# The inner rows of three feed-forward nets turned by VectorE and DRAM instead of TensorE, with three changes at the kernel's start

## The reference, cut to what matters

```python
def swiglu(x, w_gu, w_down):          # x: 256 x 1024, w_gu: 1024 x 5632, w_down: 2816 x 1024
    g, u = jnp.split(x @ w_gu, 2, axis=-1)
    return (jax.nn.silu(g) * u) @ w_down
```

## Time and profile before

| | us |
|---|---|
| median of three runs | 905.39 |
| the profiled execution | 905.16 |
| its span, first instruction to last | 903.4 |
| TensorE busy | 893.8 |
| VectorE busy | 614.2 |
| ScalarE busy | 460.2 |
| DMA, GB/s over the span | 219 |

### The profile page before, as it was taken

How to read it: one execution, slowest core, us unless ns; L and a number is a source line. 1 busy time by engine, 2 the same in 40 slices (tenths; PEclk the granted TensorE clock), 3 DMA queues, 4 the chain that set the end, 5 groups by cost and what they waited for, 6 DMA issues and landing times.

```text
span 903.4 us, 11262 instructions
## 1 busy us (share of the span) xinstructions
PE 893.8 (99%) x4208; PEld 746.9 (83%) x4208; DVE 614.2 (68%) x862; ACT 460.2 (51%) x695; POOL 42.2 (5%) x66
## 2 busy tenths in 40 slices
PE   9999999999999999999999999999999999999996
PEld 7888888888998888888888888888888888888885
DVE  6778977647558877587677777765768755555643
ACT  6675543626588466447544444454445344444530
POOL 0010000022103000000000000001000100000000
PEclk9999999999999999999999999999999999999999
DMA  9897778774554444444687777765755565555531
GB/s 360 327 347 279 275 268 295 265 226 150 187 176 173 172 179 163 163 164 154 229 292 279 280 264 279 282 246 172 248 187 166 198 219 187 186 187 186 184 120 47
DMA packets 56575, 197.83 MB, mean 219 GB/s; under 512 B 6936, under 2 KB 7880, under 8 KB 56392
## 3 DMA queue, kind: packets, MB, share of 16 engines
q1 hardware_dynamic: 55944, 196.19, 62.5%
q10 hardware_dynamic: 576, 0.92, 0.3%
HBM read 196.01 MB, written 1.07 MB: 218 GB/s over the span
## 4 chain that ended last, share of the span: by engine, by line
PE 96%; DVE 2%; issue 1%; ACT 0%; DMA 0%; POOL 0%; POOLq 0%; ACTq 0%
PE ps L708 29%; PE ps L710 29%; PE ps L709 29%; PE ps L735 2%; PE ps L646 1%; PE ps L623 1%; PE ps L834 1%; PE ps L850 1%; PE ps L616 1%; DVE t_wl L1183 0%; PE ps L792 0%; PE ps L826 0%; PE ps L774 0%; DMA t_acc<-in_xT 0%; PE ps L841 0%
## 5 line engine op out<-in xcount | busy, mean ns | idle before, releaser
L1183 DVE TENSOR_TENSOR t_wl<-t_raw,t_wh 128x1024 fp32r<-128x1024 f32 (+3 forms) x308 | 361.2, 1204 | 106.5 <-ACT t_wh L892 104.5
L892 ACT ACTIVATE t_wh<-t_raw 128x1024 fp32r<-128x1024 f32 (+3 forms) x308 | 307.4, 1040 | 87.4 <-DMA t_raw<-in_f_up 39.2
L708 PE MATMUL ps<-t_wh,t_XH 128*128 128x512 f32 (+2 forms) x640 | 250.7, 392 | 0.0
L710 PE MATMUL ps<-t_wh,t_XL 128*128 128x512 f32 (+2 forms) x640 | 247.1, 386 | 0.0
L709 PE MATMUL ps<-t_wl,t_XH 128*128 128x512 f32 (+2 forms) x640 | 246.7, 386 | 0.0
L710 PEld LDWEIGHTS ps<-t_wh,t_XL 128*128 128x128 f32 x640 | 120.1, 188 | 24.3
L709 PEld LDWEIGHTS ps<-t_wl,t_XH 128*128 128x128 f32 x640 | 120.3, 188 | 22.5
L708 PEld LDWEIGHTS ps<-t_wh,t_XH 128*128 128x128 f32 x640 | 120.2, 188 | 22.4
L708 PE MATMUL ps<-t_wh,t_YH 128*128 128x512 f32 x288 | 113.5, 394 | 0.2 <-DVE t_YL L1603 0.2
L710 PE MATMUL ps<-t_wh,t_YL 128*128 128x512 f32 x288 | 112.2, 390 | 0.0
L709 PE MATMUL ps<-t_wl,t_YH 128*128 128x512 f32 x288 | 112.1, 389 | 0.0
(11 more groups left out here) (227 smaller groups left out, 629.2 us busy)
## 6 DMA issues: line engine op xcount, KB each, us to landing
t_raw<-in_f_up SPq DMA_DIRECT2D x131, 512.0 KB, 4.0
t_raw<-in_f_dn SPq DMA_DIRECT2D x66, 512.0 KB, 3.6
t_raw<-in_ada SPq DMA_DIRECT2D x48, 512.0 KB, 3.6
t_raw<-in_mkv SPq DMA_DIRECT2D x8, 512.0 KB, 3.5
t_raw<-in_ga SPq DMA_DIRECT2D x8, 512.0 KB, 3.2
t_raw<-in_gc SPq DMA_DIRECT2D x8, 512.0 KB, 3.2
t_raw<-in_gb SPq DMA_DIRECT2D x8, 512.0 KB, 3.7
t_raw<-in_wo SPq DMA_DIRECT2D x8, 512.0 KB, 3.2
```

Source lines behind the costliest of these rows:

```text
L708: pe.matmul(o, xh, h, start=k == 0, stop=False)
L710: x = pe.matmul(o, xl, h, start=False, stop=k == n - 1)
L892: act.activation(wh[:, m % SPL, lo:w], raw[:, n % RAW, lo:w], ACT.Copy).then_inc(hi_made, 1)
L1183: dve.tensor_tensor(wl[:, n % RAW, lo:w], raw[:, n % RAW, lo:w], wh[:, m % SPL, lo:w].bitcast(F32), ALU.subtract).then_inc(drained, 1)
```

## The change

The step `hid_turn` is gone. In its place stand four steps per four groups (q = 0 to 5, the last with two half-size groups that are left):

- `blocks` on DVE: one `transpose` instruction turns `hp` (now 128 x 1024 for two groups and both row blocks) into `tp`, within blocks of 32x32 only.
- `spill` on SP: four DMAs, one for each band of 32 partitions, write `tp` to a buffer in DRAM (512 KB).
- `reload` on SP: one DMA reads it back with the bands spread so that 128 inner rows stand on partitions, into `tp`. It waits for `spilled`.
- `inner` on ACT and DVE: two copies for `HH` and two subtractions for `HL`, now read from `tp` in SBUF.

For q = 0 to 4 `spill` stands at unit 8q+8, `reload` at 8q+9, `inner` at 8q+12 (43 for q = 4); for q = 5 at 44, 45 and 48. A DMA's run is 128 values, 512 bytes (256 bytes for q = 5). The rows of the downward weights are put in a matching order on the host. At the start, ACT's queue now fetches unit 1 too, the unused transposes are 15 instead of 12, ACT's first instruction is a SiLU, and the row statistics, the first group's SiLU and the conditioning row come one step earlier.

```diff
+    def inner(f, u):
+        return [(step, f, q) for q in range(6) for step, late in (("spill", 0), ("reload", 1), ("inner", 3 if q == 4 else 4))
+                if u == (8 * q + 8 if q < 5 else 44) + late]
...
-                own = [("hid_turn", f, g - 2), ("hid_turn", f, g - 1)] if g and g % 2 == 0 and i == 2 else []
-                unit(f"{f}_up{g}", i, *own, *extra.get(4 * g + i, ()))
+                unit(f"{f}_up{g}", i, *inner(f, 4 * g + i), *extra.get(4 * g + i, ()))
             if (f, g) != ("f1", 0):
                 S.append(("hid", f, g))
+            if g % 2 or g == 10:
+                S.append(("blocks", f, g // 2))
...
-                for _ in range(12):
+                for _ in range(15):
                     pe.transpose(ps[:, 3, 0:P], ident[:, :], ident[:, :])
...
-            def hid_turn(f, g):
-                s = g % 2
-                b = bank(("hid", f, g), *hid_lo.at(f, g))
-                for t in (0, 1):
-                    pe.wait_ge(*hid_made.at(f, g, t))
-                    for c in (0, 1):
-                        m = pe.transpose(ps[:, b, c * 256 + t * P:c * 256 + t * P + P], hp[:, s, t, c * P:c * P + P], ident[:, :])
-                m.then_inc(turned, 1)
...
+                name, i = STREAM[1]
+                act.dma_start(raw[:, 1, :], A[name][i]).then_inc(landed[1], 16)
...
-                act.activation(col("first"), mhalf[:, 0:1], ACT.Copy)
+                act.activation(col("first"), mhalf[:, 0:1], ACT.Silu)
...
+            def inner(f, q):
+                act.wait_ge(reloaded, 16 * (inner_no(f, q) + 1))
+                for t in (0, 1):
+                    act.activation(parts_of(HH, q, t), placed(q, t), ACT.Copy).then_inc(*hid_hi.by(f, q, t))
...
+            def blocks(f, q):
+                n = inner_width(q) // 2
+                dve.wait_ge(*hid_made.at(f, 2 * q + (q < 5), 1))
+                dve.transpose(tp[:, 0:2 * n].rearrange("p (t n) -> p t n", t=2), hp[:, :, 0:n]).then_inc(*blocked.by(f, q))
+            def inner(f, q):
+                for t in (0, 1):
+                    dve.wait_ge(*hid_hi.at(f, q, t))
+                    dve.tensor_tensor(parts_of(HL, q, t), placed(q, t), parts_of(HH, q, t).bitcast(F32),
+                                      ALU.subtract).then_inc(*hid_lo.by(f, q, t))
...
+            def spill(f, q):
+                n = inner_width(q)
+                sp.wait_ge(*blocked.at(f, q))
+                for i in range(4):
+                    rows = inner_rows[i, :, :, 0:n // 8].rearrange("b f e -> f b e")
+                    sp.dma_start(rows, tp[32 * i:32 * i + 32, 0:n].rearrange("f (b e) -> f b e", b=8)).then_inc(spilled, 16)
+            def reload(f, q):
+                n = inner_width(q)
+                sp.wait_ge(spilled, 64 * (inner_no(f, q) + 1))
+                rows = inner_rows[:, :, :, 0:n // 8].rearrange("i (t j) f e -> (j f) (i t) e", t=2)
+                sp.dma_start(tp[:, 0:n].rearrange("p (b e) -> p b e", b=8), rows).then_inc(reloaded, 16)
```

More of the change, by code:

```diff
@@ L180, in ups @@
                     continue
[L181 to L182 removed]
+                unit(f"{f}_up{g}", i, *inner(f, 4 * g + i), *extra.get(4 * g + i, ()))
             if (f, g) != ("f1", 0):
                 S.append(("hid", f, g))
+            if g % 2 or g == 10:
+                S.append(("blocks", f, g // 2))
     def downs(f, extra, tail):
         for i in range(11):
[L188 removed]
+            unit(f"{f}_dn0", i, *inner(f, 44 + i), *extra.get(44 + i, ()))
         S.extend(rows(f, 0, 0) + rows(f, 0, 1))
@@ L502, in build @@
         silu_made, hid_made = Signal(sem("silu"), both(hid_keys)), Signal(sem("hid"), both(hid_keys))
-        hid_hi, hid_lo = Signal(sem("hid_hi"), hid_keys), Signal(sem("hid_lo"), hid_keys)
+        inner_keys = [(f, q) for f in FFNS for q in range(6)]
+        blocked = Signal(sem("blocked"), inner_keys)
+        hid_hi, hid_lo = Signal(sem("hid_hi"), both(inner_keys)), Signal(sem("hid_lo"), both(inner_keys))
+        spilled, reloaded = sem("spilled"), sem("reloaded")
         halves = steps("half")
@@ L573, in out_of, with inner_no, inner_width, placed @@
                             "ukv0": "kv0", "ukv1": "kv1"}.get(name, name), t)
+        def inner_no(f, q):
+            return 6 * FFNS.index(f) + q
+        def inner_width(q):
+            return 1024 if q < 5 else 512
+        def placed(q, t):
+            n = inner_width(q)
+            return tp[:, 0:n].rearrange("p (i t c n) -> p t c i n", i=4, t=2, n=32)[:, t]
+        def parts_of(a, q, t):
+            return a[:, 4 * q:4 * q + inner_width(q) // 256, t * P:t * P + P].rearrange("p c (i n) -> p c i n", i=4)
         def psum_2(bank):
@@ L967, in hid @@
                                    scale=r).then_inc(*silu_made.by(f, g, t))
-            def hid_turn(f, g):
-                b, full = place["hid", f, g]
-                act.wait_ge(turned, full)
-                act.activation(HH[:, 2 * g:2 * g + 2, :], psum_2(b), ACT.Copy).then_inc(*hid_hi.by(f, g))
+            def inner(f, q):
+                act.wait_ge(reloaded, 16 * (inner_no(f, q) + 1))
+                for t in (0, 1):
+                    act.activation(parts_of(HH, q, t), placed(q, t), ACT.Copy).then_inc(*hid_hi.by(f, q, t))
             def squares(p, j, t):
@@ L1298, in hid @@
                     if g >= 2 and t == 0:
-                        dve.wait_ge(turned, place["hid", f, g - 2][1])
+                        dve.wait_ge(*blocked.at(f, g // 2 - 1))
                     if f == "f3":
@@ L1619, in _ @@
             part = {"split": split, "ada": ada, "xpart": xpart, "front": front, "mem_part": mem_part, "rope1": rope1, "rope2": rope2, "rope3": rope3, "rope5": rope5, "ada_sum": ada_sum, "ada_rows": ada_rows,
-                    "hid": hid, "hid_turn": hid_turn, "half": half, "rms": rms, "gain": gain, "scaled": scaled_, "nturn": nturn, "nsplit": nsplit,
+                    "hid": hid, "blocks": blocks, "inner": inner, "half": half, "rms": rms, "gain": gain, "scaled": scaled_, "nturn": nturn, "nsplit": nsplit,
                     "xturn2": xturn2, "mk_stat": mk_stat, "lat_stat": lat_stat, "lat_row": lat_row, "lat_turn": lat_turn,
@@ L1747, in consts_ @@
                 fetch_x(1, 1)
-                for n in range(1, RAW):
+                fetch_x(2, 2)
+                for n in range(2, RAW):
                     if n < 4:
@@ L1825, in _ @@
                     "load_cond": load_cond, "ada_rows": ada_rows, "load_mod": load_mod,
-                    "load_mid": load_mid, "gate": gate, "load_final": load_final, "final": final}
+                    "load_mid": load_mid, "gate": gate, "load_final": load_final, "final": final, "spill": spill, "reload": reload}
             for name, *args in SCHEDULE:
@@ L1863, in ffn @@
             add(f"{tag}_up{j}", np.concatenate([g[:, j], u[:, j]], 1))
-        halves(f"{tag}_dn", down)
+        down, n = f(down), 5 * 512
+        quads = down[:n].reshape(5, 4, 4, 32, D).transpose(0, 2, 1, 3, 4).reshape(n, D)
+        last = down[n:].reshape(4, 2, 32, D).transpose(1, 0, 2, 3).reshape(256, D)
+        halves(f"{tag}_dn", np.concatenate([quads, last], 0))
     a["x"] = f(i["x"])[0].reshape(2, P, D)
```

22 lines of the change are left out of this document (9 added, 13 removed).

## The result

The changed kernel takes 895.01 us (median of 4 runs, 894.64 to 895.74), the kernel before 905.28 us beside it (4 runs, 904.44 to 905.69). The ratio is 0.9889 with a 95% interval of 0.9872 to 0.9906: 10.3 us faster, and 5.2 us slower than the forecast of 889.8. That is outside the forecast's own 888.0 to 892.0, and 0.5 us inside the upper end of the wide range. The profiled execution has a span of 892.9 us against 903.4.

What follows compares the result with a forecast made beforehand. TensorE, busy 893.8 of 903.4 us, was taken as the bound. 905.16 - 14.5 + 0.5 - 1.6 = 889.6, and 0.23 us to the median: 889.8 us, own range 888.0 to 892.0, wide range (8 in 10) 887.0 to 895.5.

Steps and rivals of the forecast that it cites:

- step A: On TensorE in all three nets: removing the transposes of the inner rows saves 14.5 us.
- VectorE's transpose at 1.2 us and its cover: On VectorE: the 128x1024 transpose takes 1.2 us (bounds 0.9 and 2.4), hidden behind the matmuls, cost 0.
- the middle of the nets: Away from the start of f1: ScalarE's wait for the reload and SP's blocked fetches cost 0.
- 12 us of slots: With `ada`, a refetch 18 us ahead, less landing and both splits, leaves 12 us as cushion.
- Rival 1: In f1 and f2: transfers become the bound at 341 GB/s, some 6 us lost, 896 us; chance 0.13.
- the empty stretch of 2.4 us: In each cycle: at most 2.4 us in which the DMA queue may stand empty while SP waits for written rows.
- step B: Beginning of f1, unit 17: 5.2 us of delay against 4.3 in hand, 0.5 us lost (bounds 0 and 5).
- 4.3 us in hand: At unit 17 of f1: VectorE had it at 50.5 us, TensorE takes it at 54.8, before the change.
- step C: At the start: TensorE's clock rises earlier for three more transposes, 1.6 us less (bounds 0 and 2.4).

Runs made afterwards that it cites:

- the doubled spill: The changed kernel with each spill of f2 and f3 written twice, the second copy to DRAM rows nobody reads: 897.91 us, ratio 0.9919.

## Why the prediction was right or wrong

**Right: step A, 14.5 us from TensorE.** The leads show it, fifteen steps of 0.87 to 0.89 us and three of 0.45, and eight units take 21.8 us in all three nets. That TensorE's busy time fell by 14.5 us too is partly chance: the earlier clock at the start took some 1.3 us off it and the half clock at unit 17 put 1.7 on. With the stand out of the way the whole of it arrives: the kernel with nothing of `q` = 0 of f1 on the queue is 904.79 - 889.00 = 15.8 us faster, which is A and some 1.3 us from the start and small parts. The Trainium skill's rule in "VectorE: DVE Perf Modes", section "Rules for kernel authors", to use TensorE for a 128x128 transpose if a PSUM destination will do, would have kept these 14.5 us in the time; the measurement decides against it where TensorE is the bound.

**Right: VectorE's transpose at 1.2 us and its cover.** Rows by form of the changed kernel:

```profile
L1332 DVE STREAM_TRANSPOSE t_tp<-t_hp 128x1024 f32<-128x1024 f32 x15 | 18.7, 1245 | 0.5
...
L1332 DVE STREAM_TRANSPOSE t_tp<-t_hp 128x512 f32<-128x512 f32 x3 | 2.1, 711 | 0.1
```

1.245 us. The forecast put f1's fullest stretch at 21.7 of 21.8 us; it has 21.45, and TensorE waits for nothing in it.

**Right: the middle of the nets, though with less to spare than forecast.** The spill's parts land after 3.4 us and the reload after 5.2 (forecast: 2.4 to 4, and 4, and under 5 as a sign). ScalarE waited 34.2 us for the reload in 14 times, 2.4 us in the mean and 9.3 at the longest, more than the 0 to 2 us of the forecast; no unit of TensorE behind unit 18 came late for it. The forecast compared this with 4.11 us as the longest wait for TensorE's turn; that is the longest in the rows shown, and over the whole kernel before it was 5.4 us, in 18 waits of 67.9 us. The small packets were priced about right: the queue's busy time rose from 0.625 x 903.4 to 0.697 x 892.9 us of 16 engines, 924 us x engine, for 38,160 packets more: 24 ns each, where 30 had been taken. The cycle was forecast at 341 GB/s and the rows say 346 and 349 in f1, 334 in f2. What was too high is the cushion in f2: the forecast counted 12 us of slots, the trace shows 5.3 us in the middle of the net and 3.2 at the tightest unit, and the doubled spill used it up. Rival 1 (transfers the bound) did not come true, but it was closer than its 0.13 with "12 us less 12" made it look.

By the limit of some 358 GB/s for one core in the Trainium skill ("DMA: Bandwidth & Descriptors", section "Bandwidth") and the empty stretch of 2.4 us each cycle would have been 1.4 us too long. The cycles had no wait. At 334 to 349 GB/s they lie under that figure and do not test it by themselves, but the changed kernel moved 417 GB/s in the row from 56.6 to 60 us above. The same section of the Trainium skill gives some 358 GB/s as the share when both cores of a domain stream, and 425 for one alone; the rows agree with the latter.

**Wrong: step B, the supply of f1, taken as 0.5 us and measured at 6.0.** The place, the unit and the mechanism were named; the size was not. The prediction compared 4.3 us in hand with 5.2 us of new delay, the bytes and TensorE's earlier arrival, and booked 0.5. What it had wrong:

- SP's own wait at the spill was not in the sum at all, only in its upper bound, and there by half. SP stood 4.8 us, since the product it waits for stood behind the conditioning row. Alone it makes unit 17's low part 3.1 us later. This is the step that failed.
- The bytes were taken as 2.7 us and are worth 2.7 us alone: right. But both together make it 6.7 us later, 0.9 more than their sum.
- The stand brought the clock down: 3.4 us at 1.2 GHz, 1.7 us more. The prediction priced a wait as its length.

With SP's 3.1 us in it the sum would have been 8.3 us against 4.3, 4.0 late, near the upper bound of 5 that was given. The mistake was to go near the lower end of 0 to 5, although the sign of SP's wait is known: the code makes SP wait for a product, and the trace of before has that product late. SP issued the memory rows, which the spill now precedes, from 32.45 on, and VectorE made the product only at 34.36:

```profile
34.36 0.87 DVE L1304 SCALAR_TENSOR_TENSOR t_hp<-ps,t_sc,t_sg 128x256 f32<-128x256 f32 x2
```

**Half right: step C, 1.6 us at the start.** The mechanism holds: in the changed kernel the first unit's matmuls were 0.23 us apart from 6 us on, and unit 4 started at 16.83 instead of 18.29, 1.46 us earlier, against 1.6 forecast. But alone it measured 0.7 us in the time. In one profiled execution the clock rose only at 11.1 us with the same fifteen transposes, when the first unit's high part came late and TensorE stood 0.61 us before it. And in the changed kernel it was worth nothing, since what TensorE gained it stood longer at unit 17. The forecast added C to B as if they were independent; the prediction had itself counted C against the 4.3 us in hand, and then booked it as a gain all the same.

**The sum.** By the table of leads: the start 1.46, fifteen pairs and three single groups 14.6, small parts 0.5, less 4.79 and 1.33 at units 17 and 18, is 10.4 of the 10.5 us by which the span fell. The forecast had 1.6, 14.5, nothing, and 0.5 us. That 895.01 us still lies inside 887.0 to 895.5 owes something to luck: the range reached that high for rival 1, transfers as the bound in f1 and f2, and what took the time was one stand of TensorE.

**A version that beats both.** The first inner group two units later: 889.86 us, 5.1 us under the changed kernel, with everything computed; with the conditioning row early as well 889.77, which can't be told from it. 0.8 to 0.9 us over the kernel without that group is all that is left there. The small loads stay where they are in it. Moving them only moved the stand; what stays open is how such a load would have to be written to cost less, which no run tried.

## What to carry to other kernels

When work is moved from the bound engine to queues, the steady state is the easy part; look for the one fetch that has the least time in hand, and add up every delay that the change puts ahead of it, the new waits of the issuing engine among them, before deciding that it "about fits". Delays that cost under 1 us alone cost 6 us together once the cushion is gone, and a gain upstream of such a place is worth nothing until it is mended. To measure such delays, compare when the fetched data is ready, not how long the bound engine waits. An issuing queue that is made to wait for a product should do so where that product is long made: two units later was nearly the whole repair.

## What the runs showed of the hardware that was not expected

- The norm rows, the positions and the rotation's row are 48 KB and less each, and yet while they land the 16 DMA engines stand nearly idle: 0.04 of the time and 5 GB/s from 42.5 to 44.5 us in the kernel before, 0.03 and 3 GB/s from 48.3 to 49.5 in the changed one, against 421 and 424 GB/s once the fetches behind them run. The packets in these stretches are the 64-byte ones of the two loads that copy one row of 16 values to 128 partitions. Moved away from it, the five loads gave unit 17's fetch 3.2 us back.
- The issue of the DMA that followed a spill, the memory rows and a reload on SyncE's queue took 2.76 to 4.25 us in seven kernels, whether it was a small load or, in the kernel with the norm rows late, a fetch of weights (2.96 us). In the kernels that leave the spill and the reload out, the same small load took 0.45 us. SP can fetch nothing meanwhile.
- A matmul stream that stood 4.3 us came back at 1.2 GHz and ran so for 3.4 us, 1.7 us more. After stands of 2.7 to 3.2 us in four kernels it came back at 2.4 GHz, fell to 1.2 GHz 0.7 to 1.1 us later and ran so for 3.4 us. At one stand of 3.7 us the clock was already down when the matmuls came back, and stayed at 1.2 GHz for the next 5.4 us. Stands of 0.9 us in f1 and 1.8 us in f2 left it at 2.4 GHz.
- The moment at which the clock rises at the start went with whether TensorE had stood just before its first matmul: 9.5 to 11.1 us behind stands of 0.59 to 0.70 us, 5.0 to 7.1 us behind 0.39 us or less, in 14 profiled executions. Twelve or fifteen transposes ahead did not decide it by themselves: one of the late ones had fifteen.
